# Latent attention's scores as single-pass products of high and low parts, with the work per head

## The reference

```python
def mla(q_down, kv_down, k_rope, cos, sin, q_norm_g, kv_norm_g, w_uq, w_ukv):
    c_q = rms_norm_2(q_down, q_norm_g)
    q = jnp.einsum('bsr,rhd->bshd', c_q, w_uq)
    q = jnp.concatenate([q[..., :QK_NOPE],
                         apply_rope(q[..., QK_NOPE:], cos[:, :, None, :], sin[:, :, None, :])], axis=-1)
    c_kv = rms_norm_2(kv_down, kv_norm_g)
    kv = jnp.einsum('bsr,rhd->bshd', c_kv, w_ukv)
    k_pe = apply_rope(k_rope, cos, sin)
    k = jnp.concatenate([kv[..., :QK_NOPE],
                         jnp.broadcast_to(k_pe[:, :, None, :], (B, S, MLA_HEADS, QK_ROPE))], axis=-1)
    v = kv[..., QK_NOPE:]
    o = causal_block_attention(q, k, v)
```

## Time and profile before

| | |
|---|---|
| median of 3 runs | 1832.57 us |
| the profiled execution | 1833.59 us, of which the span from the first to the last instruction is 1831.4 us |
| PE busy | 1759.6 us, 96% |
| PEld busy | 1424.0 us, 78% |
| DVE busy | 965.0 us, 53% |
| ACT busy | 724.1 us, 40% |
| POOL busy | 686.1 us, 37% |
| DMA | 31.4% of 16 engines for the weight stream, 197.67 MB |
| granted TensorE clock | 0.988 |
| latent attention's loop | 628.04 to 710.90 us in layer 1, 1325.62 to 1404.68 us in layer 2 |

### The profile page before, as it was taken

The page is one execution under the profiler, slowest core; times in us unless marked ns, Lnnn a source line. Parts: engine busy times, 40 slices in busy tenths (PEclk is TensorE's granted clock), DMA queues, the critical chain, the costliest instruction groups (busy, mean ns, idle before and its releaser), DMA issues. The chain is left out here.

```text
span 1831.4 us, 23403 instructions
## 1 busy us (share of the span) xinstructions
PE 1759.6 (96%) x8343; PEld 1424.0 (78%) x8349; DVE 965.0 (53%) x1746; ACT 724.1 (40%) x1244; POOL 686.1 (37%) x303
## 2 busy tenths in 40 slices
PE   6999999988999999999999999999999999999997
PEld 6877777777888766788888887888766788888886
DVE  7989688575579577633333322579665321101112
ACT  5434555623375554332213222466454232213221
POOL 2424111235430333554555555450211454444442
PEclk9999999999999999999999999999999999999998
DMA  6234001044332224355555532232211233232211
GB/s 244 81 104 138 24 25 35 24 166 135 113 104 99 76 80 137 128 207 184 185 189 201 184 139 92 81 115 93 103 35 35 69 104 101 83 106 101 93 58 47
DMA packets 56634, 197.67 MB, mean 108 GB/s; under 512 B 6993, under 2 KB 8017, under 8 KB 56530
## 3 DMA queue, kind: packets, MB, share of 16 engines
q1 hardware_dynamic: 56530, 196.26, 31.4%
HBM read 194.14 MB, written 2.10 MB: 107 GB/s over the span
## 5 line engine op out<-in xcount | busy, mean ns | idle before, releaser
L496 POOL TENSOR_TENSOR WL<-RAW,WH 128x1024 fp32r<-128x1024 f32 x234 | 590.7, 2529 | 907.7 <-ACT WH L585 568.0
L1743 PE MATMUL bank<-HH,WH 128*128 128x512 f32 x1120 | 437.0, 390 | 7.8 <-POOLq L501 5.8
L1745 PE MATMUL bank<-HH,WL 128*128 128x512 f32 x1120 | 435.9, 389 | 0.0
L1744 PE MATMUL bank<-HL,WH 128*128 128x512 f32 x1120 | 435.8, 389 | 0.0
L585 ACT ACTIVATE WH<-RAW 128x1024 fp32r<-128x1024 f32 x259 | 270.6, 1051 | 243.1 <-PE bank L1745 218.0
L1743 PEld LDWEIGHTS bank<-HH,WH 128*128 128x128 f32 x1120 | 210.2, 188 | 53.5 <-issue 10.1
L1745 PEld LDWEIGHTS bank<-HH,WL 128*128 128x128 f32 x1120 | 210.2, 188 | 43.8
L1744 PEld LDWEIGHTS bank<-HL,WH 128*128 128x128 f32 x1120 | 210.3, 188 | 43.1
L1676 DVE TENSOR_TENSOR HF<-SILU,bank 128x512 f32<-128x512 f32 x44 | 30.3, 688 | 314.2 <-PE bank L1745 311.2
L1743 PE MATMUL bank<-HDH,WH 128*128 128x512 f32 x352 | 137.1, 389 | 0.0
L1745 PE MATMUL bank<-HDH,WL 128*128 128x512 f32 x352 | 136.9, 389 | 0.0
(11 more groups left out here) (363 smaller groups left out, 2871.1 us busy)
## 6 DMA issues: line engine op xcount, KB each, us to landing
RAW<-in_stream SPq DMA_DIRECT2D x363, 512.0 KB, 3.3
out_t<-YA SPq DMA_DIRECT2D x8, 256.0 KB, 2.2
X<-in_xt SPq DMA_DIRECT2D x3, 512.0 KB, 8.7
X<-in_xt SPq DMA_DIRECT2D x2, 256.0 KB, 3.9
RAW<-in_stream SPq DMA_DIRECT2D x2, 256.0 KB, 4.2
ACC<-in_pos SPq DMA_DIRECT2D x1, 256.0 KB
gains<-in_gains SPq DMA_DIRECT2D x1, 224.0 KB
CS<-in_cs SPq DMA_DIRECT2D x1, 128.0 KB
```

Of the source, the lines that this page charges most:

```text
L496: nc.gpsimd.tensor_tensor(lo(k)[:], raw(k)[:], hi(k)[:].bitcast(F32), ALU.subtract).then_inc(sem["passed"], mark("passed", *k))
L1743: nc.tensor.matmul(out, A[0], B[0], start=first, stop=False)
L1744: nc.tensor.matmul(out, A[0], B[1], start=False, stop=False)
L1745: return nc.tensor.matmul(out, A[1], B[0], start=False, stop=last)
```

## The change

The scores are no longer two full-precision products, but five single-pass ones: three for the nope part (high and low of query and key, as in the dense stages), two for the rotary part. For the latter a head's turned query stands in QRS with its high part in rows 0 to 63 and its low part in rows 64 to 127, against the key's high part repeated in both halves (KPH), then its low part repeated (KPL); GpSimd's zeroed tiles go. High parts are made by ScalarE, low parts by VectorE, from the bank, per head: rotary query (4 transposes of its own), nope query, nope key of head h+1, in the steps of units (h, 0), (h, 1), (h, 2), each after the rest of the step's work. Head 0's are made before the loop. Some tiles move in memory.

```diff
-        QRT = w("QRT", [P, 4, S], F32, 48)
-        QN = w("QN", [P, 2, S], F32, 56)
-        KN = w("KN", [P, 2, S], F32, 60)
-        KPE = w("KPE", [P, 2, S], F32, 64)
+        QNH = w("QNH", [P, 2, S], F32R, 48)
+        QNL = w("QNL", [P, 2, S], F32R, 52)
+        KNH = w("KNH", [P, 2, S], F32R, 56)
+        KNL = w("KNL", [P, 2, S], F32R, 60)
+        QRS = w("QRS", [P, 2, S], F32R, 64)
+        KPH = w("KPH", [P, S], F32R, 68)
+        KPL = w("KPL", [P, S], F32R, 70)
...
-                pool.wait_ge(sem["ya_gated"], value("ya_gated", layer, KD - 1))
-                pool.wait_ge(sem["passed"], max(1, count["passed"]))
-                nc.gpsimd.memset(KPE[DH:P, 0, :], 0.0)
-                nc.gpsimd.memset(KPE[0:DH, 1, :], 0.0).then_inc(sem["pool_set"], mark("pool_set", "kpe", layer))
-                pool.wait_ge(sem["pool_set"], value("pool_set", "kpe", layer))
...
-                nc.scalar.activation(KPE[0:DH, 0, :], b[0:DH, :], ACT.Copy)
-                nc.scalar.activation(KPE[DH:P, 1, :], b[0:DH, :], ACT.Copy).then_inc(
-                    sem["read_act"], mark("read_act", "tc2", L, 3))
+                nc.scalar.activation(KPH[0:DH, :], b[0:DH, :], ACT.Copy)
+                nc.scalar.activation(KPH[DH:P, :], b[0:DH, :], ACT.Copy).then_inc(
+                    sem["rot_hi"], mark("rot_hi", L, "key"))
...
-                for h in range(2):
-                    evict(QN[:, h, :], "qn", L, h, scale=float(QK) ** -0.5)
-                for i in range(4):
-                    evict(QRT[:, i, :], "tq", L, i)
+                def query_rot(h):
+
+                    act.wait_ge(sem["full"], value("full", "tq", L, h))
+                    nc.scalar.activation(QRS[0:DH, h % 2, :], bank_of("tq", L, h)[0:DH, :], ACT.Copy).then_inc(
+                        sem["rot_hi"], mark("rot_hi", L, h))
+
+                def query_nope(h):
+
+                    act.wait_ge(sem["full"], value("full", "qn", L, h))
+                    nc.scalar.activation(QNH[:, h % 2, :], bank_of("qn", L, h)[:], ACT.Copy,
+                                         scale=float(QK) ** -0.5).then_inc(sem["qn_hi"], mark("qn_hi", L, h))
+
+                def key_nope(h):
+
+                    act.wait_ge(sem["full"], value("full", "kn", L, h))
+                    nc.scalar.activation(KNH[:, h % 2, :], bank_of("kn", L, h)[:], ACT.Copy).then_inc(
+                        sem["kn_hi"], mark("kn_hi", L, h))
+
+                query_nope(0)
+                key_nope(0)
+                query_rot(0)
...
-                        if qt == 1 and 1 <= h < HEADS - 1:
+                        if qt == 0 and 1 <= h < HEADS - 1:
                             split_through(("hd", L, 3) if h > 1 and L == 0 else ("hd", L, (h + 1) // 2),
                                           0 if L == 0 and h > 1 else SPLIT_RING - 1 - (L == 0))
-                            act.wait_ge(sem["full"], value("full", "s", 2 + L, 4 * (h - 1) + 3))
-                            evict(QN[:, (h + 1) % 2, :], "qn", L, h + 1, scale=float(QK) ** -0.5)
+                        if h < HEADS - 1:
+                            if h and qt == 0:
+                                act.wait_ge(sem["full"], value("full", "s", 2 + L, 4 * (h - 1) + 3))
+                            if qt < 3:
+                                (query_rot, query_nope, key_nope)[qt](h + 1)
...
+                dve.wait_ge(sem["rot_hi"], value("rot_hi", L, "key"))
+                b = bank_of("tc2", L, 3)
+                for rows in (slice(0, DH), slice(DH, P)):
+                    ins = V.tensor_tensor(KPL[rows, :], b[0:DH, :], KPH[0:DH, :].bitcast(F32), ALU.subtract)
+                ins.then_inc(sem["read_dve"], mark("read_dve", "tc2", L, 3))
...
+                def query_rot_lo(h):
+
+                    dve.wait_ge(sem["rot_hi"], value("rot_hi", L, h))
+                    V.tensor_tensor(QRS[DH:P, h % 2, :], bank_of("tq", L, h)[0:DH, :],
+                                    QRS[0:DH, h % 2, :].bitcast(F32), ALU.subtract).then_inc(
+                        sem["read_dve"], mark("read_dve", "tq", L, h))
+
+                def query_nope_lo(h):
+
+                    dve.wait_ge(sem["qn_hi"], value("qn_hi", L, h))
+                    V.scalar_tensor_tensor(out=QNL[:, h % 2, :], in0=bank_of("qn", L, h)[:], scalar=float(QK) ** -0.5,
+                                           in1=QNH[:, h % 2, :].bitcast(F32), op0=ALU.mult,
+                                           op1=ALU.subtract).then_inc(sem["read_dve"], mark("read_dve", "qn", L, h))
+
+                def key_nope_lo(h):
+
+                    dve.wait_ge(sem["kn_hi"], value("kn_hi", L, h))
+                    V.tensor_tensor(KNL[:, h % 2, :], bank_of("kn", L, h)[:], KNH[:, h % 2, :].bitcast(F32),
+                                    ALU.subtract).then_inc(sem["read_dve"], mark("read_dve", "kn", L, h))
+
+                query_nope_lo(0)
+                key_nope_lo(0)
+                query_rot_lo(0)
...
-                            dve.wait_ge(sem["full"], value("full", "s", 2 + L, 4 * (h - 1) + 3))
-                            dve.wait_ge(sem["full"], value("full", "kn", L, h + 1))
-                            b = bank_of("kn", L, h + 1)
-                            V.tensor_copy(KN[:, (h + 1) % 2, :], b[:]).then_inc(
-                                sem["read_dve"], mark("read_dve", "kn", L, h + 1))
+                        if h < HEADS - 1 and qt < 3:
+                            (query_rot_lo, query_nope_lo, key_nope_lo)[qt](h + 1)
...
-                def head_qk(hd):
+                def rotated(hd):
+
+                    turn(("tq", L, hd), [QRR[:, tt, hd * DH:(hd + 1) * DH] for tt in range(NT)], rows=DH)
+
+                def nope_query(hd):
 
                     slot = ("hd", L, hd // 2)
                     c = 3 * P * (hd % 2)
...
                     for k in range(2):
                         last = mm3(b[:], wpair(slot, c + P * k, P), (CQH[:, k, :], CQL[:, k, :]), k == 0, k == 1)
                     full(last, "qn", L, hd)
+
+                def nope_key(hd):
+
+                    slot = ("hd", L, hd // 2)
+                    c = 3 * P * (hd % 2)
                     b = claim("kn", L, hd)
                     full(mm3(b[:], wpair(slot, c + 2 * P, P), (CKH[:], CKL[:]), True, True), "kn", L, hd)
                     used(slot)
 
-                head_qk(0)
-                head_qk(1)
+                nope_query(0)
+                nope_key(0)
                 pe.wait_ge(step, value("q_roped", L))
-                for i in range(4):
-                    turn(("tq", L, i), [QRR[:, tt, i * P:(i + 1) * P] for tt in range(NT)])
+                rotated(0)
                 nU = len(UNITS2)
                 for u in range(nU + O_LAG):
                     if u < nU:
                         hd, qt = UNITS2[u]
                         n = (qt + 1) * P
                         if u == 0:
-                            pe.wait_ge(sem["pool_set"], value("pool_set", "kpe", L))
-                            pe.wait_ge(sem["read_act"], value("read_act", "tq", L, 3))
-                            pe.wait_ge(sem["read_act"], value("read_act", "tc2", L, 3))
-                        pe.wait_ge(sem["read_act"], value("read_act", "qn", L, hd))
-                        pe.wait_ge(sem["read_dve"], value("read_dve", "kn", L, hd))
+                            pe.wait_ge(sem["read_dve"], value("read_dve", "tc2", L, 3))
+                        if qt == 0:
+                            for kind in ("qn", "kn", "tq"):
+                                pe.wait_ge(sem["read_dve"], value("read_dve", kind, L, hd))
                         b = claim("s", 2 + L, u)
-                        nc.tensor.matmul(b[:, 0:n], QN[:, hd % 2, qt * P:(qt + 1) * P], KN[:, hd % 2, 0:n],
-                                         start=True, stop=False)
-                        nc.tensor.matmul(b[:, 0:n], QRT[:, hd // 2, qt * P:(qt + 1) * P], KPE[:, hd % 2, 0:n],
-                                         start=False, stop=False)
+                        q, i = slice(qt * P, (qt + 1) * P), hd % 2
+                        mm3(b[:, 0:n], (QNH[:, i, q], QNL[:, i, q]), (KNH[:, i, 0:n], KNL[:, i, 0:n]), True, False)
+                        nc.tensor.matmul(b[:, 0:n], QRS[:, i, q], KPH[:, 0:n], start=False, stop=False)
+                        nc.tensor.matmul(b[:, 0:n], QRS[:, i, q], KPL[:, 0:n], start=False, stop=False)
...
-                        if qt == 1 and 1 <= hd < HEADS - 1:
-                            head_qk(hd + 1)
+                        if hd < HEADS - 1 and qt < 3:
+                            (rotated, nope_query, nope_key)[qt](hd + 1)
...
```

More of the change, by code:

```diff
@@ L180 @@
     "ya_gated", "c_hi", "y_full", "y_hi", "hid", "hid_hi", "x_half", "h_lo", "yb", "y_lo", "cmp_p", "xc_lo",
[L181 removed]
+    "p_norm", "hid_lo", "w_used", "gated_in", "rot_hi", "qn_hi", "kn_hi",
 )
@@ L301, in program @@
         HSQ = w("HSQ", [P, 4, S], F32, 78.25)
-        ACC3 = w("ACC3", [P, 1024], F32, 68)
```

(19 more changed lines are left out.)

1 line of the change is left out of this document (removed).

## The result

The changed kernel takes 1853.76 us, median of four runs, beside 1832.55 us for the kernel before: 21.2 us more, a quotient of 1.0116. The ratio on record, which is not that of the medians, is 1.0134, with a 95% interval of 1.0115 to 1.0153. Forecast were 1850.6 us. The profiled execution took 1853.56 us with a span of 1851.8 us, 20.4 us more than before.

A forecast was written before the change was run, and what follows sets the result against it. A serial ring of three engines, not TensorE's work, was to bound the loops: +7.5 us (layer 2), +11.7 (layer 1), -1.2 ahead of them, +18.0 on 1833.59, 1851.6; the median 1.0 lower, 1850.6 us; range 1843 to 1859.

The forecast's parts named there:

- The bound: Latent attention loops: a plain head is set by waits among three engines, 10.1 us, where TensorE now needs 9.89.
- the ring: Serial chain in each head through VectorE, ScalarE and the product of probabilities and values, without TensorE's scores: 10.1 us.
- A plain head: Head without weight split or scaling in the chain, such as layer 2's heads 2, 4, 6: 10.1 us.
- one with a split: Layer 2's heads 3 and 5: 10.1 us plus 0.94 for ScalarE's weight split, 11.05 each.
- layer 1's long ones: Layer 1's heads with two scalings of 1.05 us in the chain: 12.7, 12.8 and 12.2 us.
- VectorE's idle time in front of the rotary low part: In a plain head VectorE is free after 1.39 us, ScalarE's rotary high part done after 1.89: 0.5 us idle.
- TensorE's part: Narrow single-pass products and added turns: 7.5 us less work a layer, 15 in all, 9.1 us a head.
- rival (c): Narrow products also run at four passes: about +2 us, or +8 (1858.5) with 256 columns too; chance 13%.
- One sign named in advance: In the two loops, TensorE's work was to be down 7 to 8 us a loop.
- The front: Ahead of each loop: start 1.1 us earlier, 0.5 given back by the key's low parts, net -0.6 a layer.
- The sum: Both loops and what precedes them: 7.5 + 11.7 - 1.2 = +18.0 us.
- Rival (d): TensorE's clock falls to half after waits up to 3.6 us; two or three falls give 1857 to 1860; chance 12%.

The follow-up runs named there:

- kernel 1: The changed kernel with two of the five products of each score unit left out; ratio 1.0188 against the kernel before.
- 6: The changed kernel with two of five score products left out and products that serve nothing put into TensorE's waits; ratio 1.0144 against the kernel before.
- 11: The changed kernel's steps reordered on all three engines, waits filled with products that serve nothing, two of five score products left out; ratio 0.9922.
- kernels 3: The changed kernel with each low part made one unit later on VectorE, behind the next row maximum; ratio 1.0093 against the kernel before.
- 7: The changed kernel with low parts one unit later and high parts ahead of weight split and scaling; ratio 1.0080 against the kernel before.
- 8: The changed kernel's whole computation, reordered on TensorE, ScalarE and VectorE so that no engine waits for a part just asked for; ratio 0.9979.
- kernel 12: The changed kernel with products that serve nothing in TensorE's waits, layer 2's list of them corrected; ratio 1.0108 against the kernel before.
- kernel 4: The changed kernel with ScalarE's high parts made ahead of the weight split and the scaling; ratio 1.0176 against the kernel before.
- the new order: The changed kernel's whole computation, its steps reordered on TensorE, ScalarE and VectorE; ratios 0.9979 and, run again, 0.9971 against the kernel before.
- the new order with fillers: The reordered whole computation with products that serve nothing in TensorE's waits outside of the steady heads; ratio 0.9953 against the kernel before.

## Why the prediction held, step by step

**The bound.** The step that mattered, that TensorE's score products are nowhere in the ring, is shown from both sides by kernels 1, 6 and 11, and that its order makes it by kernels 3, 7 and 8. A plain head was put at 10.1 us and takes 10.21; one with a split at 11.05 and takes 11.16; layer 1's long ones at 12.7, 12.8 and 12.2 and take 12.78, 12.79 and 11.97 where the clock holds (kernel 12). VectorE's idle time in front of the rotary low part, 0.5 by the working, is 0.40; in front of the nope-query one it is 0.73. That a split stands in the ring because it delays the rotary high part is borne out by that low part's wait, 1.35 us with a split and 0.40 without one. That moving it would take its time away was not in the prediction but in the expectation of kernel 4, and failed because GpSimd's hold on the normalisation took its place.

**TensorE's part.** The prices taken for narrow products, 0.11 and 0.122 us, are the measured ones, so rival (c) is out; only the first product of a unit takes longer to the second, 0.14 us at 128 columns and 0.20 at 256. Its work in a head was put at 9.1 us; where it sets the pace, in the new order, a head takes 9.25. The 15 us of work that TensorE was to lose are then some 12 to 13, and in the main they were there to be had: the new order with fillers holds the whole of the change's work and beats the kernel before by 9 us. One sign named in advance did not show: TensorE's work was to be down 7 to 8 us a loop, and its busy time rose from 76.30 and 76.04 us to 78.73 and 77.39. The sign left out that part of the former front's work now lies in the loops; besides, a lowered clock lengthens the records and a record before a wait counts in full, so busy time does not measure this.

**The front.** Forecast was a gain of 0.6 us a layer. From the first nope query to the first score it took 6.89 us in both layers before, 6.76 and 7.09 now: no gain, 1.2 us of the sum wrong. TensorE's first score waits 1.70 us (1.60 in layer 2) for the rotary low part, which stands behind two other low parts on VectorE.

**The sum.** Loops and fronts were to cost 18.0 us and cost 24.1. The front is 1.2 of that, and 3.1 are falls of the clock, by kernel 12's windows. The rest, 1.8 us, are tenths in heads of both loops (ring steps of 10.2 for 10.1, last heads of 13.7 for 13.4). Outside of the two stages this execution is 3.7 us shorter than the one of before (2.5 ahead of layer 1's stage, 1.3 between the two), where the change touches little; the clock's falls in those stages differ between executions. So the span grew by 20.4, not 24.1. That the total came out within 3.2 us of the forecast is in part luck: the loops and fronts alone are 6 us off, and the other stages took 3.7 of it back.

**Rival (d).** The case that came true is the ring together with (d). It was given 12% and two or three falls at 1857 to 1860; there were five lowered stretches, but much of what they cost was hidden in waits, and they were worth 3 to 5 us by kernel 12 (a difference of the ratios that is not clear of noise; the windows give the 3), not 6 to 9. What was wrong is the size of (d): a fall costs only where the rest waits for the slow products, as for the product of probabilities and values at 1421.21, which had waited only 0.90 us just before it. Its condition was sized wrongly as well: it had been tied to single waits of up to 3.6 us, but in head 0 the clock is 0.81 and 0.79 behind waits of 2.2 and 1.7 us (layer 2: 2.2 and 1.6) ahead of the loop, with none over 1 us inside the head.

The Trainium skill (TensorE: Matmul & The Clock Gate, "What's actually happening") says that the throttled clock is the array's default and that activity releases it; the 0.87 of kernel 1, which waits longer, and the 1.00 of kernel 12, whose waits are filled, agree.

**What stays open.** The hold on VectorE's normalisation while GpSimd works was seen again in the change (the 128-column one at 1350.00 took 2.22 us, beside 0.29 at 1361.32, with two splits under way on GpSimd), and kernel 4 made more of it, but no run took it away by itself, so what it costs the change is not known. Layer 1's last head, 16.1 us against 13.7 in layer 2, was not taken apart.

## What to carry to other kernels

When an operand becomes two parts made on two engines, follow the new dependency once around both queues before counting the matrix work: the part to be waited for belongs one unit behind the request, not beside it. If the busiest engine waits in such a ring, taking work from it gains nothing and may cost time through its clock; first reorder the ring, then lighten the engine. When a step is moved out of such a ring, see what it starts on other engines: kernel 4's split, moved, let GpSimd hold VectorE instead. A cheap test of which of the two, the ring or the busiest engine, sets the pace is to leave work out on that engine, in the old order and in the new.

## What the runs showed of the hardware

Less work made the kernel slower: 20 us of products left out, 10 us more time, the loops' granted clock from 0.95 and 0.96 down to 0.87 and 0.91. Products that serve nothing, put into the waits, gave 8 of the 10 us back (1.0144 for 1.0188).

A pair of 64-row products among those of 128 costs about 0.1 us at each of three steps, into the pair, between the two and out of it (0.32, 0.33 and 0.33 us for 0.23 at 512 columns), though they read half the rows: stacking the rotary pair's two parts in 128 rows saves that too, about 1 us a head.

The normalisation of a 128-column tile took 2.22 us while GpSimd split two weight tiles, 2.23 us when it began 0.25 us behind the start of one such split (kernel 4), and 0.29 with GpSimd idle.
